# Expert weight tiles with longer rows: gate and up in blocks of 1024 inner columns, down tiles of two adjacent inner rows a partition

## The reference

```
D_MODEL = 1024
D_FF = ((8 * D_MODEL // 3 + 255) // 256) * 256
def swiglu(x, wg, wu, wd):
    return jnp.dot(jax.nn.silu(jnp.dot(x, wg)) * jnp.dot(x, wu), wd)
    ...
    for e in range(N_EXPERTS):
        y = y + gate[:, e:e + 1] * swiglu(xf, wg[e], wu[e], wd[e]).astype(jnp.float32)
```

## Time and profile before

| | us |
|---|---|
| median of three runs | 1248.1 (1248.07 to 1249.15) |
| the profiled execution, whole | 1249.45 |
| its span, first to last instruction | 1247.7 |
| PE busy in the span | 1206.4 (97%) |
| DVE busy | 975.4 (78%) |
| ACT busy | 807.1 (65%) |
| queue of the weight loads, share of 16 DMA engines | 75.1% |

### The profile page before, as it was taken

How to read it: one execution, slowest core, us unless ns; L and a number is a source line. 1 busy time by engine, 2 the same in 40 slices (tenths; PEclk the granted TensorE clock), 3 DMA queues, 4 the chain that set the end, 5 groups by cost and what they waited for, 6 DMA issues and landing times.

```text
span 1247.7 us, 16144 instructions
## 1 busy us (share of the span) xinstructions
PE 1206.4 (97%) x6567; PEld 1045.6 (84%) x6567; DVE 975.4 (78%) x907; ACT 807.1 (65%) x875; POOL 31.9 (3%) x40
## 2 busy tenths in 40 slices
PE   6999999999998989999999999999999999999996
PEld 4899999999997878888888888888888888888885
DVE  6787444447898559889888888888888888888887
ACT  4545654436596448768767777777777777777771
POOL 0000000000000000001001001001001001001000
PEclk9999999999999979999999999999999999999998
DMA  9144544442193439999999999999999999999991
GB/s 257 41 151 153 169 145 160 141 156 90 53 318 107 135 110 327 366 366 359 385 371 359 388 368 356 393 374 358 391 367 348 394 376 342 394 380 344 395 345 50
DMA packets 171388, 345.74 MB, mean 277 GB/s; under 512 B 7042, under 2 KB 59618, under 8 KB 171274
## 3 DMA queue, kind: packets, MB, share of 16 engines
q1 hardware_dynamic: 168515, 335.34, 75.1%
q0 software_dynamic: 2592, 8.66, 2.8%
q10 hardware_dynamic: 199, 0.62, 0.2%
HBM read 336.34 MB, written 10.44 MB: 278 GB/s over the span
## 4 chain that ended last, share of the span: by engine, by line
PE 87%; DVE 9%; ACT 2%; DMA 1%; issue 1%; POOLq 0%; ACTq 0%; POOL 0%; DVEq 0%
PE bank L1243 39%; PE bank L1267 19%; PE bank L1075 18%; PE bank L1106 6%; DVE cacc L1517 3%; PE bank L1252 1%; PE bank L1014 1%; PE bank L1211 1%; DVE w_lo L1334 1%; DMA spool<-in_state_pool_dram 1%; PE bank L1060 1%; DVE sg L1414 1%; ACT w_hi L683 0%; ACT sq L727 0%; DVE cacc L1538 0%
## 5 line engine op out<-in xcount | busy, mean ns | idle before, releaser
L1334 DVE TENSOR_TENSOR w_lo<-raw,w_hi 128x2048 fp32r<-128x2048 f32 x309 | 704.5, 2290 | 164.8 <-ACT w_hi L683 163.8
L683 ACT CAST w_hi<-raw 128x2048 fp32r<-128x2048 f32 x309 | 589.5, 1916 | 243.2 <-PE bank L1243 81.3
L1243 PE MATMUL bank<-w_hi,xg_hi 128*128 128x512 f32 (+1 forms) x768 | 292.1, 380 | 1.1 <-DVE xg_lo L1715 1.1
L1243 PE MATMUL bank<-w_hi,xg_lo 128*128 128x512 f32 (+1 forms) x768 | 288.6, 376 | 0.0
L1243 PE MATMUL bank<-w_lo,xg_hi 128*128 128x512 f32 (+1 forms) x768 | 288.6, 376 | 0.0
L1075 PE MATMUL bank<-x_hi,w_hi 128*128 128x304 f32 (+1 forms) x544 | 166.8, 307 | 6.9 <-DVE x_lo L1421 3.7
L1243 PEld LDWEIGHTS bank<-w_hi,xg_hi 128*128 128x128 f32 x768 | 144.2, 188 | 29.2 <-issue 1.3
L1243 PEld LDWEIGHTS bank<-w_hi,xg_lo 128*128 128x128 f32 x768 | 144.2, 188 | 29.1
L1243 PEld LDWEIGHTS bank<-w_lo,xg_hi 128*128 128x128 f32 x768 | 144.4, 188 | 28.0
L1075 PE MATMUL bank<-x_lo,w_hi 128*128 128x304 f32 (+1 forms) x544 | 165.1, 304 | 0.0
L1075 PE MATMUL bank<-x_hi,w_lo 128*128 128x304 f32 (+1 forms) x544 | 164.5, 302 | 0.0
(11 more groups left out here) (206 smaller groups left out, 1097.0 us busy)
## 6 DMA issues: line engine op xcount, KB each, us to landing
raw<-in_moe_w_gate_dram SPq DMA_DIRECT2D x88, 1024.0 KB, 7.0
raw<-in_moe_w_up_dram SPq DMA_DIRECT2D x88, 1024.0 KB, 7.4
raw<-in_moe_w_down_dram SPq DMA_DIRECT2D x88, 1024.0 KB, 7.1
raw<-in_conv_w_dram SPq DMA_DIRECT2D x12, 1024.0 KB, 5.2
raw<-in_ffn_w_gate_dram SPq DMA_DIRECT2D x11, 1024.0 KB, 5.3
raw<-in_ffn_w_up_dram SPq DMA_DIRECT2D x11, 1024.0 KB, 5.3
raw<-in_ffn_w_down_dram SPq DMA_DIRECT2D x11, 1024.0 KB, 4.8
sums_dram<-acc SPq DMA_DIRECT2D x3, 512.0 KB, 3.0
```

Of the source, the lines that this page charges most:

```text
L683: act.copy(w_hi[t % HIGH][:], raw[raw_slot(t)][:]).then_inc(hi_ready, 1)
L1243: done = pe.matmul(bank[:, 0:w], x[:, f, :], m[:, c, :], start=(f == 0 and k == 0), stop=(f == KC - 1 and k == 2))
L1334: dve.tensor_tensor(w_lo[raw_slot(t)][:], raw[raw_slot(t)][:], w_hi[t % HIGH][:], ALU.subtract).then_inc(split_ready, 1)
```

## The change

Gate and up are cut into blocks of 1024, 1024, 512 and 256 columns. A tile of a 1024-block holds 256 input rows of 1024 columns (4 KB each), and the block's output takes two banks: gate has bank 0 and 1, up bank 2 and 3, each in every block. Each row chunk of a tile is multiplied in two parts of 512 columns (`parts`). Down tiles give a partition the inner rows 2p and 2p + 1, which are adjacent in memory (one run of 8 KB); to match, the transposes read `hn` with a step of two elements (`hn_rows`). The buffers `hn`, `sgn`, `ht_hi` and `ht_lo` double in size.

```
-    NB = NJ // 2 + 1
-    BW = 2 * TW
+    SIZES = (4,) * (NJ // 4) + (2,) * (NJ % 4 // 2) + (1,) * (NJ % 2)
+    NB = len(SIZES)
+    BW = 4 * TW
...
+        hn_rows = hn[:, :].rearrange("p (i m s) -> p i s m", s=TR, m=P)
...
+        FIRST = [sum(2 * k for k in SIZES[:b]) + sum(SIZES[:max(b - 1, 0)]) for b in range(NB)]
         def halves(b):
-            return 2 if b < NB - 1 else 1
+            return SIZES[b]
+        def parts(b):
+            w = TW * SIZES[b]
+            return (512, 512) if w == 1024 else (w,)
...
-                    cols = slice(b * BW, min((b + 1) * BW, F))
+                    rows = D // halves(b)
+                    r0 = at_tile % halves(b) * rows
+                    view = {4: pairs, 2: quad, 1: wide}[halves(b)]
+                    c0 = TW * sum(SIZES[:b])
+                    cols = slice(c0, c0 + TW * halves(b))
...
-                return src.rearrange("o (c p) f -> p (o c) f", p=P), tall
+                return src.rearrange("o (p c) f -> p (o c) f", p=P), tall
...
                         for c in range(chunks):
                             f = half * chunks + c
-                            for k, (x, m) in enumerate(((xg_hi, wh), (xg_hi, wl), (xg_lo, wh))):
-                                done = pe.matmul(bank[:, 0:w], x[:, f, :], m[:, c, :],
-                                                 start=(f == 0 and k == 0), stop=(f == KC - 1 and k == 2))
+                            for part, w in enumerate(parts(j)):
+                                cols = slice(part * 512, part * 512 + w)
+                                for k, (x, m) in enumerate(((xg_hi, wh), (xg_hi, wl), (xg_lo, wh))):
+                                    done = pe.matmul(ps[bank + part][:, 0:w], x[:, f, :], m[:, c, cols],
+                                                     start=(f == 0 and k == 0), stop=(f == KC - 1 and k == 2))
...
-                        done = pe.transpose(ps[4 + j % 2][:, s * P:(s + 1) * P], hn[:, s * P:(s + 1) * P], ident[:])
+                        done = pe.transpose(ps[4 + s // 4][:, s % 4 * P:(s % 4 + 1) * P], hn_rows[:, s // TR, s % TR, :],
+                                            ident[:])
...
-                    pe.wait_ge(silu_done, n * NB + (FC + max(0, j - 1)))
-                    rows_block(ps[(j + 1) % 2], j, g)
+                    pe.wait_ge(silu_done, n * NB + (FC + j))
+                    rows_block(0, j, g)
...
-                    pe.wait_ge(h_done, n * NB + (FC + max(0, j - 1)))
-                    rows_block(ps[2 + (j + 1) % 2], j, g + halves(j))
+                    pe.wait_ge(h_done, n * NB + (FC + j))
+                    rows_block(2, j, g + halves(j))
```

More of the change, by code:

```diff
@@ L222, in build_trunk @@
         hn = area("hn", [P, BW], F32, M1 + 8192)
-        sgn = area("sgn", [P, BW], F32, M1 + 10240)
-        ht_hi = area("ht_hi", [P, 2 * TR, P], F32R, M1 + 12288)
-        ht_lo = area("ht_lo", [P, 2 * TR, P], F32R, M1 + 14336)
+        hn_rows = hn[:, :].rearrange("p (i m s) -> p i s m", s=TR, m=P)
+        sgn = area("sgn", [P, BW], F32, M1 + 12288)
+        ht_hi = area("ht_hi", [P, 4 * TR, P], F32R, M0 + 16384)
+        ht_lo = area("ht_lo", [P, 4 * TR, P], F32R, M0 + 20480)
         yy = area("yy", [P, D], F32, 0)
@@ L360, in quad, with pairs @@
             return t[:, :].rearrange("p (k f) -> p k f", k=KC // 2)
-        FIRST = [0] + [6 * b - 2 for b in range(1, NB)]
+        def pairs(t):
+            return t[:, :].rearrange("p (k f) -> p k f", k=2)
+        FIRST = [sum(2 * k for k in SIZES[:b]) + sum(SIZES[:max(b - 1, 0)]) for b in range(NB)]
         def halves(b):
-            return 2 if b < NB - 1 else 1
+            return SIZES[b]
+        def parts(b):
+            w = TW * SIZES[b]
+            return (512, 512) if w == 1024 else (w,)
         def gate_end(b):
@@ L480, in expert_tile @@
                     w = (moe_w_gate, moe_w_up)[at_tile // halves(b)]
[L481 to L484, removed]
-                    cols = slice(b * BW, min((b + 1) * BW, F))
+                    rows = D // halves(b)
[3 more added lines that the diff above has]
+                    cols = slice(c0, c0 + TW * halves(b))
                     return w[0, bass.ds(e, 1), r0:r0 + rows, cols].rearrange("o (c p) f -> p (o c) f", p=P), view
-                i = 2 * (b - 1) + at_tile - 2 * halves(b)
+                i = sum(SIZES[:b - 1]) + at_tile - 2 * halves(b)
                 src = moe_w_down[0].rearrange("e (j r) f -> (e j) r f", r=TW)[bass.ds(e * NJ + i, 1)]
-                return src.rearrange("o (c p) f -> p (o c) f", p=P), tall
+                return src.rearrange("o (p c) f -> p (o c) f", p=P), tall
             def load_expert(n, e, j):
@@ L905, in silu @@
                 def silu(j):
-                    w = halves(j) * TW
                     act.wait_ge(tile_used, t0 + (T_MOE + gate_end(j) + 1))
                     act.wait_ge(h_done, n * NB + (FC + j))
-                    act.activation(sgn[:, 0:w], ps[(j + 1) % 2][:, 0:w], ACT.Silu).then_inc(silu_done, 1)
+                    for part, w in enumerate(parts(j)):
+                        last = act.activation(sgn[:, part * 512:part * 512 + w], ps[part][:, 0:w], ACT.Silu)
+                    last.then_inc(silu_done, 1)
                 def turn_evac(j):
-                    k = halves(j) * TR
                     act.wait_ge(h_turned, n * NB + (j + 1))
-                    act.copy(ht_hi[:, 0:k, :], ps[4 + j % 2][:, 0:k * P].rearrange("p (c n) -> p c n", c=k))\
-                        .then_inc(ht_hi_done, 1)
+                    for part, w in enumerate(parts(j)):
+                        k = w // P
+                        last = act.copy(ht_hi[:, 4 * part:4 * part + k, :],
+                                        ps[4 + part][:, 0:w].rearrange("p (c n) -> p c n", c=k))
+                    last.then_inc(ht_hi_done, 1)
                 for j in range(NB):
                     a = FIRST[j] + AHEAD
-                    ahead(a)
-                    if halves(j) == 2:
-                        ahead(a + 1)
+                    for k in range(halves(j)):
+                        ahead(a + k)
                     silu(j)
@@ L924, in one_expert @@
                         turn_evac(j - 1)
-                    if halves(j) == 2:
+                    for k in range(halves(j)):
+                        ahead(a + halves(j) + k)
+                    if j == NB - 1:
                         ahead(a + 2)
[L927 to L933, removed]
+                    elif j:
+                        for k in range(halves(j - 1)):
+                            ahead(a + 2 * halves(j) + k)
                 if kept:
@@ L1236, in rows_block @@
                         if j == 0:
-                            pe.wait_ge(xg_lo_done, n * 2 + (half + 1))
-                        view, chunks = (quad, KC // 2) if halves(j) == 2 else (wide, KC)
+                            pe.wait_ge(xg_lo_done, n * 2 + (half // 2 + 1))
+                        view = {4: pairs, 2: quad, 1: wide}[halves(j)]
+                        chunks = KC // halves(j)
                         wh, wl = view(w_hi[t % HIGH]), view(w_lo[raw_slot(t)])
@@ L1730, in mult @@
                 def mult(j):
-                    w = halves(j) * TW
                     dve.wait_ge(silu_done, n * NB + (FC + j + 1))
                     dve.wait_ge(tile_used, n * TE + (T_MOE + up_end(j) + 1))
-                    dve.tensor_tensor(hn[:, 0:w], sgn[:, 0:w], ps[2 + (j + 1) % 2][:, 0:w], ALU.mult).then_inc(h_done, 1)
+                    for part, w in enumerate(parts(j)):
+                        cols = slice(part * 512, part * 512 + w)
+                        done = dve.tensor_tensor(hn[:, cols], sgn[:, cols], ps[2 + part][:, 0:w], ALU.mult)
+                    done.then_inc(h_done, 1)
                 def turn_low(j):
-                    k = halves(j) * TR
                     dve.wait_ge(ht_hi_done, n * NB + (j + 1))
-                    dve.tensor_tensor(ht_lo[:, 0:k, :], ps[4 + j % 2][:, 0:k * P].rearrange("p (c n) -> p c n", c=k),
-                                      ht_hi[:, 0:k, :], ALU.subtract).then_inc(ht_lo_done, 1)
+                    for part, w in enumerate(parts(j)):
+                        k = w // P
+                        done = dve.tensor_tensor(ht_lo[:, 4 * part:4 * part + k, :],
+                                                 ps[4 + part][:, 0:w].rearrange("p (c n) -> p c n", c=k),
+                                                 ht_hi[:, 4 * part:4 * part + k, :], ALU.subtract)
+                    done.then_inc(ht_lo_done, 1)
                 for j in range(NB):
                     a = FIRST[j] + AHEAD
-                    ahead(a)
-                    if halves(j) == 2:
-                        ahead(a + 1)
+                    for k in range(halves(j)):
+                        ahead(a + k)
                     if j:
                         turn_low(j - 1)
[L1749 to L1753, removed]
+                    for k in range(halves(j)):
```

(9 more changed lines are left out.)

6 lines of the change are left out of this document (4 added, 2 removed).

## The result

The changed kernel takes 1251.02 us (median of 13 runs, 1249.92 to 1253.11), the kernel before 1248.78 in the 13 runs beside them (1247.98 to 1250.05). The ratio is 1.0019 with a 95% interval of 1.001 to 1.0028: 0.19% slower, inside the forecast range of 1245 to 1253 and inside the 0.2% that the prediction called no change, but 0.4 us above the range of 1247 to 1250.6 that it gave the forecast itself. The interval leaves no doubt about the sign. There is a small cost, and the study is about where it sits and what became of the quicker loads.

The account below looks back on a forecast made before the run. PE was taken to bound the experts, with loads covered. All terms were 0 except +0.7 us for transposes with a step: 1247.7 + 1.75 + 0.7 = 1250.15 profiled, 1248.8 us for the median, range 1245 to 1253.

Parts of the forecast that it names:

- The bound: Experts: PE sets the pace, busy 99.95 of 100 us; loads are covered, SP and ACT wait for PE.
- the account of one expert: One expert on PE: matmuls 86.8 and 5.6, transposes 3.3, seam 0.3; sum 96.0 us against 95.94 between experts.
- Fewer packets and an earlier landing: Expert loads: 9600 runs an expert instead of 15104, landing at or under 7 us; gain taken as 0.
- The step of two: PE's transposes of `hn`: +0.7 us over 176 transposes, the middle of 0 and +1.4.
- the nearest row: Moving read of the 256-column matmul, 1 KB a partition in 0.1168 us; at that pace transposes cost +1.4 us.
- the prediction's own signs: Profile after: eight transposes 0.87 to 0.93 us, an expert 95.9 to 96.1; transposes over 0.12 each prove a step wrong.
- The rival of slow transposes: Weight loads of `hn` in each expert's turns slow down; up to 19.2 us, 1267.3; chance 0.09.
- The rival that a single set of banks would stall PE: Silu and product lie bare after blocks; 6.5 us an expert, 52 us in all, 1300.8; chance 0.04.
- The transfers' margin: Expert loads: five tiles, 14.0 us, from issue to cast; the slowest load shown had 4.4 us to spare.
- each further microsecond would be paid on every tile: Expert loads: if a tile took longer than 14.0 us to land, each further us of tile time hits every tile.
- The level: Whole kernel: median before taken as 1248.1 us, the profiled execution 1.35 above it; 1248.8 forecast for the median.
- the 0.28 us at the seam: Between two experts PE's weight load waits 0.28 us for `ht_lo`; forecast to stay.

Follow-up runs that it names:

- the step of 8: Changed kernel with down tiles dealing a whole block's rows to the partitions, so the two large blocks read `hn` with a step of 8: 1250.26 us, before 1248.99.
- the hold of three tiles: Each expert load waits three PE tiles longer: kernel before 1257.87 us (1249.51 without), changed kernel 1251.91 (ratio 1.0024 to the kernel before).

## Why the prediction was right, and what was off

*The bound.* Right. The waits named PE as the pace and the transfers as covered, and the account of one expert from five rows closed within 0.1 us of its period; after the change the same account with the new transposes gives the new period within 0.1 us (96.0 plus 16 transposes at about 0.119 and 6 at about 0.123 instead of 0.109, 0.24 us, against 0.27 measured; the sections leave some 0.04 us an expert for the blocks). Fewer packets and an earlier landing came as forecast and gave nothing.

*The step of two.* The place was right, a read with a step that costs a little, and the term was too small. I took 0.7 us, the middle between nothing and the 1.4 us of the nearest row, with no reason for the middle. By the sections it measured 1.92 us alone and 1.97 with the blocks, 0.011 us for each of the 176 transposes; the nearest row alone would have been closer. Three of the prediction's own signs showed it: eight transposes took 0.95 us where 0.87 to 0.93 was forecast, four took 0.123 each where over 0.12 was to prove a step wrong, and an expert took 96.21 us where 95.9 to 96.1 was forecast. The rival of slow transposes was to decide from 0.0142 us a transpose on, so it came three quarters of the way. That the time still lies in the stated range is in part luck: the range had been widened towards the rivals, and the forecast's own range was missed. The rule of the Trainium skill (page "SBUF — State Buffer", section "Door 1: The DMA port swizzle"), by which a step of up to four float32 elements is free, doesn't agree with the runs: steps of 2 and 4 cost 0.008 to 0.014 us a transpose, and the step of 8, which by the rule should pay, only 0.001 to 0.002. The rival's full price of 19.2 us was far off.

*Banks.* The rival that a single set of banks would stall PE did not come true: the kernel with the blocks alone has the time of before, with 0.34 us more in its section. Here the general advice of the Trainium skill to rotate through banks (page "Perfetto Trace Analysis", section "Optimizing Tensor Performance") has nothing to save, since other tiles lie between a block's matmuls and the next use of its banks. Under the hold of three tiles the larger blocks even gave room.

*The transfers' margin.* That they are covered was right; the size of the margin was read from one chain only. I counted 14.0 us from a load's issue to its cast and 4.4 us to spare. With 8.4 us of it taken away casts waited for loads, as that count says, yet the section grew by only 9.9 us in 768: that each further microsecond would be paid on every tile was wrong, because a second cover, the six split tiles, lies behind the first. What ran out first was not the weight that PE needed next but the product in DVE's list behind it.

*The level.* 1248.8 was forecast, 1251.02 measured. The kernel before itself has 1248.78 in the larger set of runs where three runs gave 1248.1, so 0.7 of the difference is the level and 1.5 the size of the term above, with the small cost of the blocks in it.

## What to carry to other kernels

Here longer rows gave nothing, because no wait of PE ended with a load; the view to ask first is who waits for whom, since DMA engines can be full (98.2% here) with transfers that nothing waits for. When a layout is changed for the sake of loads, look which engine reads it with a step afterwards, and give the step to an engine with idle time (here DVE took it for 0 ns). An account of one period from the prices of its instructions shows what is left to gain: here it was the 0.28 us at the seam, worth more than the whole change of the loads.

## What the runs showed of the hardware that was not expected

A float32 weight load of 128 x 128 with a step of two takes 193 to 214 ns in the trace instead of 137 to 143, but only 0.008 to 0.014 us of that reaches the pace of the transposes; and the cost isn't monotone in the step (0.109 without, 0.117 to 0.123 with 2, 0.123 with 4, 0.111 with 8). A product on DVE with both float32 operands at a step of two, one of them in PSUM, took the same 680 ns as without.
